# Attention weights turned by VectorE block transposes and a trip through DRAM, in a two-layer hybrid encoder on one Trainium2 core

## The reference

```
def sink_softmax(scores, sink, mask=None):
    s = jnp.where(mask, scores.astype(jnp.float32), -jnp.inf)
    sk = jnp.broadcast_to(sink[:, :, None, None], s.shape[:-1] + (1,))
    return jax.nn.softmax(jnp.concatenate([s, sk], axis=-1), axis=-1)[..., :-1]

def swa_mixer(p, sinks, cos, sin):        # 4 query heads, 2 key/value heads of 64
...
    kb, vb = band(kr, km), band(vr, vm)   # 16 meta tokens, the chunk before, the chunk
    pr = sink_softmax(jnp.einsum('bcqkgd,bcskd->bckgqs', qr, kb), sink, valid)
    orr = jnp.einsum('bckgqs,bcskd->bcqkgd', pr.astype(v.dtype), vb)
```

## Time and profile before

| | |
|---|---|
| median of three runs | 3052.5 us (3052.41, 3052.5, 3058.36) |
| the profiled execution | 3056.32 us, of which the span is 3054.4 us |
| granted TensorE clock, mean | 0.999 of full speed |
| busy: PE, PEld, DVE, ACT, POOL | 99%, 90%, 50%, 31%, 7% of the span |
| DMA, mean over the span | 249 GB/s |

### The profile page before, as it was taken

How to read it: one execution, slowest core, us unless ns; L and a number is a source line. 1 busy time by engine, 2 the same in 40 slices (tenths; PEclk the granted TensorE clock), 3 DMA queues, 4 the chain that set the end, 5 groups by cost and what they waited for, 6 DMA issues and landing times.

```text
span 3054.4 us, 64343 instructions
## 1 busy us (share of the span) xinstructions
PE 3011.8 (99%) x27180; PEld 2759.9 (90%) x27180; DVE 1529.4 (50%) x3672; ACT 939.6 (31%) x2381; POOL 216.8 (7%) x319
## 2 busy tenths in 40 slices
PE   8999999999999999999999999999999999999998
PEld 7788778889898899989989899999999999999998
DVE  4345552355633455336554366544566255663562
ACT  3324440134421343124341144303343043421320
POOL 0111010011101110010010101000000000000000
PEclk9999999999999999999999999999999999999999
DMA  7577477788978989888797898986768857787887
GB/s 256 170 205 213 118 208 218 220 237 283 311 236 263 280 273 320 242 259 272 238 313 210 264 276 261 295 284 196 260 205 268 290 178 249 210 267 253 301 302 248
DMA packets 227116, 760.19 MB, mean 249 GB/s; under 512 B 25088, under 2 KB 44672, under 8 KB 226576
## 3 DMA queue, kind: packets, MB, share of 16 engines
q1 hardware_dynamic: 189328, 620.80, 61.6%
q0 software_dynamic: 37504, 135.28, 18.0%
HBM read 744.33 MB, written 136.31 MB: 288 GB/s over the span
## 4 chain that ended last, share of the span: by engine, by line
PE 92%; DMA 3%; DVE 3%; ACT 2%; issue 0%; SPq 0%; ACTq 0%; DVEq 0%
PE psum L1853 29%; PE psum L1306 27%; PE psum L1876 10%; PE psum L1912 8%; PE psum L1443 7%; DMA slots<-in_weights 2%; PE psum L1300 1%; PE psum L1322 1%; PE psum L1621 1%; PE psum L1646 1%; DMA slots<-wsum 1%; PE psum L1633 1%; PE psum L1572 1%; PE psum L1694 1%; PE psum L1803 1%
## 5 line engine op out<-in xcount | busy, mean ns | idle before, releaser
L1306 PE MATMUL psum<-hT,slots 128*128 128x256 f32 (+1 forms) x2880 | 658.9, 387 | 2.8 <-ACT hT L874 2.1
L1306 PEld LDWEIGHTS psum<-hT,slots 128*128 128x128 f32 x2880 | 541.6, 190 | 97.0 <-issue 5.5
L1853 PE MATMUL psum<-tsum,slots 128*128 128x128 f32 (+1 forms) x4928 | 608.0, 277 | 11.6 <-ACT raw L1223 4.9
L1853 PEld LDWEIGHTS psum<-tsum,slots 128*128 128x128 f32 x4928 | 573.1, 191 | 28.6 <-issue 20.2
L1853 PE MATMUL psum<-hT,slots 128*128 128x128 f32 (+1 forms) x3696 | 453.7, 276 | 6.9 <-DMA slots<-in_weights 3.9
L1853 PEld LDWEIGHTS psum<-hT,slots 128*128 128x128 f32 x3696 | 432.6, 192 | 10.1 <-DMA slots<-in_weights 4.9
L1876 PE MATMUL psum<-gT,slots 128*128 128x256 f32 (+1 forms) x1408 | 309.9, 383 | 0.0
L1876 PEld LDWEIGHTS psum<-gT,slots 128*128 128x128 f32 x1408 | 267.1, 190 | 40.9
L1306 PE MATMUL psum<-mixT,slots 128*128 128x256 f32 (+2 forms) x1024 | 226.4, 381 | 1.1 <-DVE hT L2030 1.1
L1306 PEld LDWEIGHTS psum<-mixT,slots 128*128 128x128 f32 x1024 | 194.3, 190 | 29.7 <-issue 1.5
L2030 DVE SCALAR_TENSOR_TENSOR hT<-hT,psum 128x256 f32<-128x256 f32 (+2 forms) x96 | 40.5, 423 | 348.3 <-PE psum L1876 249.7
(11 more groups left out here) (326 smaller groups left out, 3526.6 us busy)
## 6 DMA issues: line engine op xcount, KB each, us to landing
slots<-in_weights SPq DMA_DIRECT2D x667, 512.0 KB, 4.6
slots<-wsum SPq DMA_DIRECT2D x308, 512.0 KB, 4.5
wsum<-in_weights POOLq DMA_DIRECT2D x132, 512.0 KB, 6.7
slots<-wsumi SPq DMA_DIRECT2D x64, 512.0 KB, 4.4
slots<-wsumd SPq DMA_DIRECT2D x64, 512.0 KB, 4.5
wsum<-wsum POOLq DMA_DIRECT2D x44, 512.0 KB, 7.9
wsumi<-in_weights POOLq DMA_DIRECT2D x24, 512.0 KB, 7.5
wsumd<-in_weights POOLq DMA_DIRECT2D x24, 512.0 KB, 9.3
```

The lines of the kernel that those rows point to most:

```text
L1306: ins = mm(psum[:, i % 2, :n], lhsT, rhs, start=k == 0, stop=k == len(pairs) - 1)
L1853: ins = mm(dst[:, e * n:(e + 1) * n], w[:, (4 * e + k) * P:(4 * e + k + 1) * P], moving[s][k], start=s in (0, 1, 5) and e == 0 and k == 0, ...
```

## The change

For the twelve tiles with u >= 2 and j > 0 (two in each of units 2 to 7) the eight transposes on TensorE and ScalarE's two copies go. In their place:

- VectorE, behind its division, turns the 32 x 32 blocks of `PR` in two instructions (128 x 512 and 128 x 384) into `PC`, which shares the tile `SC` of the scores; semaphore `p_cut`.
- ScalarE at t0 + 3 waits for `p_cut` and issues one DMA of 128 x 1024 (512 KB) from `SC` to a DRAM tensor `pdram`; semaphore `p_out`.
- ScalarE at t0 + 5 waits for `p_out` and issues two loads of 32 x 4 x 256 (128 KB each) from `pdram` to `PB`, and two more at t0 + 6; semaphore `p_in`.
- TensorE at t0 + 8 waits for `p_in` and multiplies `PB` by the values; ScalarE copies the result in two instructions instead of one.

A tile takes nine steps instead of five. In a unit without meta tokens the first tile has its scores in step 9, the DMA out in 12, the loads in 14 and 15 and the values in 17; the second has scores in 18, the DMA out in 21, the loads in 23 and 24 and the values in 26. Programs chained behind `side` (the tiles of unit 3's input, the stores of finished tiles) come eight steps later. One more memset is made at the start, and the scratch for descriptors of GpSimd's DMAs is 1024 instead of 2048.

```diff
+def weights_by_blocks(u, j):
+    return u >= 2 and j > 0
...
+VALUES_STEP = 8
...
-        SC = sb("SC", 4 * WIN)[:, :].rearrange("p (h s) -> p h s", h=4)
+        sc = sb("SC", 1024)
+        SC = sc[:, 0:4 * WIN].rearrange("p (h s) -> p h s", h=4)
...
+        PC = sc[:, 0:1024].rearrange("p (q m c) -> p q m c", q=4, m=2)
+        PB = prpt[:, 1024:2048].rearrange("p (b m c) -> p b m c", b=4, m=2)
+        pdram = nc.dram_tensor("pdram", (P, 1024), F32, kind="Internal").ap()
...
+            g.memset(sc[:, 28 * BLOCK:1024], 0.0).then_inc(S["init"], 1)
...
                     yield
                     yield
-                    a.wait_ge(S["a_pt"], nth + 1)
+                    if weights_by_blocks(u, j):
+                        turn = tiles_where(weights_by_blocks, nth)
+                        a.wait_ge(S["p_cut"], turn + 1)
+                        if turn:
+                            a.wait_ge(S["p_in"], 64 * turn)
+                        a.dma_start(pdram, sc[:, 0:1024]).then_inc(S["p_out"], 16)
+                        yield
+                        yield
+                        a.wait_ge(S["p_out"], 16 * (turn + 1))
+                        by_keys = pdram.rearrange("(b s) (q c) -> q s b c", b=4, q=4)
+                        for q in range(4):
+                            a.dma_start(PB[BLOCK * q:BLOCK * (q + 1)].rearrange("p b m c -> p b (m c)"), by_keys[q]
+                                        ).then_inc(S["p_in"], 16)
+                            if q % 2:
+                                yield
+                        for _ in range(VALUES_STEP - 7):
+                            yield
+                        a.wait_ge(S["a_oT"], nth + 1)
+                        for g in range(2):
+                            ins = act(mixT[:, 2 + g, off:off + P].rearrange("p (b s) -> p b s", b=4),
+                                      bank(BX)[:, 0:2 * P].rearrange("p (b g s) -> p g b s", b=4, g=2)[:, g], ACT.Copy)
+                        ins.then_inc(S["a_mix"], 1)
+                        yield
+                        continue
+                    a.wait_ge(S["a_pt"], tiles_not(weights_by_blocks, nth) + 1)
...
                     yield
                     yield
                     yield
-                    pe.wait_ge(S["a_pn"], nth + 1)
+                    if weights_by_blocks(u, j):
+                        for _ in range(VALUES_STEP - 3):
+                            yield
+                        pe.wait_ge(S["p_in"], 64 * (tiles_where(weights_by_blocks, nth) + 1))
+                        for m in range(2):
+                            rows_m = min(w - P * m, P)
+                            for kv in range(2):
+                                ins = mm(bank(BX)[HD * kv:HD * kv + HD, 0:2 * P].rearrange("p (b c) -> p b c", b=4),
+                                         Vw[:rows_m, b, m, HD * kv:HD * kv + HD],
+                                         PB[:rows_m, :, m, 2 * BLOCK * kv:2 * BLOCK * (kv + 1)], start=m == 0, stop=m == 1)
+                        ins.then_inc(S["a_oT"], 1)
+                        yield
+                        continue
+                    pe.wait_ge(S["a_pn"], tiles_not(weights_by_blocks, nth) + 1)
...
-                    tt(PR[:n_, :, :w], PR[:n_, :, :w], rden[:n_, :, None].broadcast_to([n_, 4, w]),
-                       ALU.mult).then_inc(S["a_pn"], 1)
+                    ins = tt(PR[:n_, :, :w], PR[:n_, :, :w], rden[:n_, :, None].broadcast_to([n_, 4, w]), ALU.mult)
+                    if weights_by_blocks(u, j):
+                        after(step(ins))
+                        for m in range(2):
+                            ins = v.transpose(PC[:, 0:4 - m, m].rearrange("p q (h s) -> p q h s", h=4),
+                                              PR[:, :, P * m:P * m + P - BLOCK * m].rearrange("p h (q s) -> p q h s", s=BLOCK))
+                        ins.then_inc(S["p_cut"], 1)
+                        for _ in range(VALUES_STEP - 4):
+                            yield
+                    else:
+                        ins.then_inc(S["a_pn"], 1)
...
-    nc = bacc.Bacc("TRN2", target_bir_lowering=False, num_devices=1, dynamic_dma_scratch_size=2048)
+    nc = bacc.Bacc("TRN2", target_bir_lowering=False, num_devices=1, dynamic_dma_scratch_size=1024)
```

More of the change, by code:

```diff
@@ L116 @@
 DN_BLOCKS = 3
+ALL_TILES = [(u, j) for u in range(NU) for j, _, _ in tiles_of(u)]
 DN_SLOTS = 8 * DN_BLOCKS
@@ L124, with keys_by_blocks, tiles_where, tiles_not @@
 SWA_PART = ["sq0", "sq1", "sk", "sv"]
+def keys_by_blocks(u, j):
+    return u > 0 and j > 0
+def weights_by_blocks(u, j):
+    return u >= 2 and j > 0
+def tiles_where(test, nth):
+    return sum(test(*tile) for tile in ALL_TILES[:nth])
+def tiles_not(test, nth):
+    return nth - tiles_where(test, nth)
 def input_part(u):
@@ L443, in build @@
         dsum = wset[:, 0:4 * KH * P].rearrange("p (j k t) -> p j k t", j=4, k=KH)
-        PR = prpt[:, 0:4 * WIN].rearrange("p (h s) -> p h s", h=4)
+        PR = prpt[:, 0:28 * BLOCK].rearrange("p (h s) -> p h s", h=4)
+        PC = sc[:, 0:1024].rearrange("p (q m c) -> p q m c", q=4, m=2)
+        PB = prpt[:, 1024:2048].rearrange("p (b m c) -> p b m c", b=4, m=2)
+        pdram = nc.dram_tensor("pdram", (P, 1024), F32, kind="Internal").ap()
         PT = prpt[:, 1024:2048].rearrange("p (m h s) -> p m h s", m=2, h=4)
@@ L515, in build @@
             "r_tr", "r_kc", "r_vc", "r_sc", "r_sm", "r_state", "r_o", "r_oc", "r_ssq", "r_sd", "r_mix",
-            "a_kept", "a_window", "a_vt", "a_vtc", "a_sc", "a_scm", "a_max", "a_exp", "a_es", "a_pn", "a_pt", "a_ptc",
+            "a_kept", "a_window", "a_vt", "a_vtc", "a_sc", "a_scm", "a_max", "a_exp", "a_es", "a_pn", "p_cut", "p_out", "p_in", "a_pt", "a_ptc",
             "a_oT", "a_mix",
@@ L1798, in side @@
                     yield
-                    pe.wait_ge(S["a_ptc"], nth + 1)
+                    pe.wait_ge(S["a_ptc"], tiles_not(weights_by_blocks, nth) + 1)
                     for m in range(2 if j else 1):
@@ L2774, in end_step @@
                     scale_tile(0, 2)
-            v.wait_ge(S["init"], 5)
+            v.wait_ge(S["init"], 6)
             rest(*(input_tile(j) for j in range(3)))
```

## The result

The changed kernel takes 1.0043 times the time before, 95% interval 1.0026 to 1.006: some 13 us slower, with an interval of 8 to 18 us (medians of five runs each 3069.84 and 3055.44 us; one run of 6377.93 us counts in the first median, but is left out of the ratio). Its profiled execution has a span of 3064.1 us, 9.7 more than before.

A forecast was written before the change was run, and what follows sets the result against it. TensorE, busy in 99% of the span with 92% of the chain, was taken as the bound. Transposes -11.2, issues +7.6 and other DMAs +2 gave -1.6 us from 3052.5: about 3051 us, range 3041 to 3063.

The forecast's parts named there:

- +2 us: Other DMAs, mostly beside up(1) to up(4): 16 added transfers make weight slots late, about 1 us, doubled; bounds 0 and 29.
- margin 1.3 us, so 0: Second tile's last loads land at 2705.9, 1.3 us before the values need them, so TensorE waits 0.
- -11.2 us: TensorE's list, twelve tiles: eight transposes leave each, 12 x 0.93 us less.
- the 0.93: Unit 7, second tile: distance from the turn's start to the next block, taken as TensorE's loss to eight transposes.
- Issues, +7.6 us: ScalarE, second tile's two pairs of loads: issues delay copies of products in units 2, 3, 5, 6, 7; bounds 2.2 and 11.2.
- the 1.51: Delay a unit from the second tile's load issues on ScalarE: 0.69 us for the first pair plus 0.82 for the second.
- 0.06 us a transfer: Present price of DMA contention: 10.2 us of slot waits over 176 transfers for `wsum`, applied to 16 added transfers.
- Scratch, 0: Smaller scratch for descriptors of GpSimd's DMAs: costed at 0, as no trace row shows GpSimd waiting for it.
- VectorE's block transposes, 0: VectorE behind its division: about 1.08 us a tile of transposes, hidden in idle time, costed at 0.
- the 1.12 us: VectorE's idle time, waiting for ScalarE's copy in unit 7's first tile, taken to absorb the block transposes' delay.
- 0.66 us stall: TensorE's loss at 2658.97 behind a copy made late by the second tile's exponentials: moves four steps down, 0 net.
- Rival B: Beside up(1) to up(4) full DMA engines land the store late and ScalarE waits for `p_out`: 3059 to 3069 us, chance 0.22.

The follow-up runs named there:

- without a trip: Changed kernel without its DMA out and four loads, stale weights multiplied: 0.9974; in the old five steps 0.9972; in units 2 to 5 alone 0.998.
- the pad: Kernel before with scratch 1024 instead of 2048 and an unused tile of 1024 bytes ahead of all others: 0.9992.
- the small trip: Changed kernel with the same one store and four loads a tile, but 8 columns instead of 1024: 0.9996, -1.2 us.
- one load: Changed kernel with four stores and one load a tile instead of one store and four loads, same bytes: 1.0001; in units 6 and 7 alone 0.9982.
- values later: Changed kernel with the values nine steps behind the scores instead of eight, second tile one step later too: 1.0011.

## Why the prediction was wrong

It forecast 3051 us with a range of 3041 to 3063, and no change that can be measured as the likeliest class (0.44); it is 13 us slower. The steps that failed are the prices of the DMAs: "+2 us" for what the others lose was 8.3, and "margin 1.3 us, so 0" for the last loads was 6.9 us of waiting. The gain of -11.2 us was too large as well. By its own steps:

- **Transposes, -11.2 us: too large.** In units 6 and 7 two turns free 1.46 and 1.45 us, so 0.73 a tile; the 0.93 is the distance at one turn, and not what the unit gains. Twelve tiles at 0.73 make 8.8. In unit 3 the gain is as large: up(2), from its first block to the first of down(2), lasts 176.4 us in all five kernels with the smaller scratch and the old code there, and 174.9 and 175.0 in the two without a trip in nine steps. In unit 4 VectorE takes it back (below). In units 2 and 5 traces of the same code differ by up to 3 us (up(1) 182.1 to 184.6, up(4) 178.9 to 181.9), more than the gain, so it can't be read there. That TensorE's saved time turns into slot waits is not shown: those are 9.9 and 8.9 us without a trip, 10.2 before, though 7.8 and 6.9 with the smaller scratch and the pad. With the scratch in them the no-trip kernels gain 8.0 and 8.6 us.
- **Issues, +7.6 us: right in mechanism, in size by luck** (6.8 us by the small trip, of which one 3.0 us wait is for a load). A pair takes 0.31 + 0.45 us as a rule, not 2 x 0.61, but in the full kernel single issues last up to 1.50 us, and one such row alone costs 1.3 us in unit 7. In the quiet units without such a row a unit pays 0.8 us, half of the 1.51.
- **"Margin 1.3 us, so 0" for the last loads: failed.** TensorE waits 6.9 us for loads, in seven of the twelve tiles, first tiles among them: the longest, 2.8 us, is in unit 2's. The duration was read from SyncE's `raw<-rows`, 3.1 us, which never leaves SBUF; the loads from DRAM land after 5.8 us, up to 11.9. SyncE's slots, which also come from DRAM to SBUF, have 4.5; already that would have left no margin (2702.8 + 4.5 = 2707.3 against 2707.16).
- **"+2 us" for the other DMAs: off by a factor of four.** 8.3 us between no trip and the same bytes with one load. The price of 0.06 us a transfer was a mean over transfers that the kernel before had placed so that they mostly fit; the next bytes in such a stretch (a share of 1.01 in up(4)) cost about 1 us a MB. Doubling the mean was a guess. In the changed kernel itself the slot waits rise by 1.6 us only. A reading that fits is that TensorE loses its time at the copies and the values first, which gives the slots time: with these mended they are 16.9 (one load) and 19.0 (values later).
- **Scratch, 0: off**, by 2.4 to 5.5 us in the change's favour; the smaller of the two is not clear of 0.
- **VectorE's block transposes, 0: failed in unit 4**, by 2.4 us. Nobody waits for `p_cut`, and a transpose has 0.625 us in the median (forecast 0.62 and 0.46). But the prediction read its cover in one tile of unit 7, and there the 1.12 us stand behind four other instructions, not right behind the division as the heading of the earlier trace rows has it. In unit 4 `rwkv`'s sums stand there, and TensorE waits for them; VectorE's timeline, then TensorE's:

```profile
1616.13 1.17 DVE L2648 STREAM_TRANSPOSE SC<-prpt 128x512 f32<-128x512 f32 x2
...
1620.23 0.49 DVE L2485 TENSOR_TENSOR wset<-wset,small 128x128 f32<-128x128 f32 x2
```

```profile
1620.82 0.45 PE L1568 MATMUL psum<-Zb,wset 64*64 64x64 f32 x8 [1.56 <-DVE wset L2485]
```

The division, in its new place, stands ahead of the transposes, so the 1.56 us are not theirs alone. The memset shows no wait. The second tile's exponentials moved their 0.66 us stall along, as forecast.

The sum that the runs give: -8.0 (no trip: transposes, VectorE's part and scratch) + 8.3 (bytes) + 12.8 (four loads in place of one: issues and late loads) = +13.1. It has to come out, since each term is the step from one kernel to the next; what it shows is the sizes, against -11.2, +2 and +7.6 forecast.

Rival B had the side right, and its 3059 to 3069 us hold the measured time, but by luck: the wait that it names, ScalarE's for `p_out`, didn't occur. The store lands after 4.7 to 9.8 us, and ScalarE asks for it no sooner than 10.4 us after the issue, so `p_out` kept nobody waiting: two steps are longer than four blocks, since the steps of `rwkv` lie between them. The late DMAs were the loads, and TensorE waited for them, not ScalarE.

The Trainium skill (DMA: Bandwidth & Descriptors, Issuing engines are not separate DMA queues) says that a DMA of another issuing engine runs on the same 16 DMA engines and saves sequencer time alone. The runs agree: though ScalarE's queue is new and all its own, its bytes make SyncE's slots late, 16.9 us of waits for them instead of 9.9.

Of the kernels with the whole computation, the form with one load in units 6 and 7 is the best, 0.9982 (0.9972 to 0.9993) of before; the scratch alone, 0.9982, can't be told from it. By its rows 2.9 us of it are the two units' transposes.

## What to carry to other kernels

Ask for each stretch apart what sets its pace: where the DMA engines were full, the trip cost about 1 us a MB, and where they had room, nothing. Price work that moves to another engine at each place where it stands, and not at one: VectorE's was free in unit 7 and cost 2.4 us in unit 4. Place the DMAs that an engine issues by what stands behind them in its list, and have the reordering done on the side of the trip that has idle time: one load instead of four at the tight step was worth 12.8 us at equal bytes. For a landing time take the row with the same source and target memory, and look at its largest value beside its median.

## What the runs showed that I had not expected

- ScalarE issues a DMA while its own activation is executing, 0.01 us behind its start; a load behind another one takes 0.45 us where the first takes 0.31, and now and then 0.7 to 1.5 us. What lengthens it no row shows; the small trip has one of 1.88 us, so it is not the load's own bytes.
- Of the three sizes of the scratch for GpSimd's descriptors the middle one is the best for this kernel: 2048 is 2.4 to 5.5 us slower than 1024, and 512 is 25 us slower than 2048, with 60 to 100 us of "issue" ahead of each of six DMA lines of GpSimd.
- Stretches beside up(1) and up(4) scatter by up to 3 us from trace to trace with the same code, while up(2) agrees within 0.1 us in five traces and units 6 and 7 within 0.1 us. Up(3) seems to scatter when the kernel before is set beside the scratch alone (4.8 us), but five traces with 1024 lie together and the one with 2048 apart. A difference of a few us in a stretch can be read only beside traces of the same code.
